# Attention with stick-breaking weights: the softplus of key blocks 2 and 3 is summed on VectorE, and one product serves both

## The reference, cut to what matters

```
neg_log_keep = jnp.where(mask, jax.nn.softplus(z), 0.0)
rcs = lax.cumsum(neg_log_keep, axis=3, reverse=True)
suffix = jnp.concatenate([rcs[..., 1:], jnp.zeros_like(rcs[..., :1])], axis=-1)
a = jnp.where(mask, jnp.exp(jax.nn.log_sigmoid(z) - suffix), 0.0)
return jnp.einsum('bhqk,bhkd->bhqd', a, vf)
```

## Time and profile before

| | us |
|---|---|
| median of 3 runs | 1982.65 (1981.83 to 1983.25) |
| the profiled execution | 1983.95 |
| its span | 1982.2 |
| TensorE busy | 1948.1 (98%) |
| VectorE busy | 1106.1 (56%) |
| ScalarE busy | 661.3 (33%) |
| GpSimd busy | 149.5 (8%) |
| mean granted TensorE clock | 0.993 |

### The profile page before, as it was taken

The page is one execution under the profiler, slowest core; times in us unless marked ns, Lnnn a source line. Parts: engine busy times, 40 slices in busy tenths (PEclk is TensorE's granted clock), DMA queues, the critical chain, the costliest instruction groups (busy, mean ns, idle before and its releaser), DMA issues.

```text
span 1982.2 us, 24091 instructions
## 1 busy us (share of the span) xinstructions
PE 1948.1 (98%) x9454; PEld 1568.1 (79%) x9454; DVE 1106.1 (56%) x1344; ACT 661.3 (33%) x742; POOL 149.5 (8%) x101
## 2 busy tenths in 40 slices
PE   6999999999999999999999999999999999999999
PEld 4888888876578888888888888888778788888887
DVE  3866564589887565633665533345569774333222
ACT  3422322242254323232432322223248743322211
POOL 0100000121411000001100000111012020000000
PEclk8999999999989999999999999999999999999999
DMA  9454544436413545433254422233235323222222
GB/s 394 163 211 171 206 167 162 161 103 183 125 59 133 212 170 201 167 123 101 107 212 172 188 99 76 99 119 114 85 93 137 112 85 106 85 106 85 88 97 91
DMA packets 50777, 275.88 MB, mean 139 GB/s; under 512 B 7456, under 2 KB 8096, under 8 KB 25760
## 3 DMA queue, kind: packets, MB, share of 16 engines
q1 hardware_dynamic: 47648, 270.87, 38.7%
q10 hardware_dynamic: 3072, 4.23, 0.9%
HBM read 251.94 MB, written 2.10 MB: 128 GB/s over the span
## 4 chain that ended last, share of the span: by engine, by line
PE 90%; DVE 4%; ACT 2%; DMA 2%; issue 1%; SPq 0%; ACTq 0%; DVEq 0%
PE ps L1420 27%; PE ps L1421 26%; PE ps L1422 26%; PE ps L1662 2%; PE ps L1441 2%; DMA stage<-ada_d 1%; PE ps L1796 1%; PE ps L1810 1%; PE ps L1782 1%; PE ps L1448 1%; DVE w L864 1%; PE ps L1549 1%; PE ps L1461 1%; PE ps L1460 1%; PE ps L1466 1%
## 5 line engine op out<-in xcount | busy, mean ns | idle before, releaser
L1420 PE MATMUL ps<-h_hi,w 128*128 128x512 f32 x1552 | 609.6, 393 | 0.1
L1422 PE MATMUL ps<-h_hi,w 128*128 128x512 f32 x1552 | 604.2, 389 | 0.0
L1421 PE MATMUL ps<-h_lo,w 128*128 128x512 f32 x1552 | 604.1, 389 | 0.0
L1420 PEld LDWEIGHTS ps<-h_hi,w 128*128 128x128 f32 x1552 | 291.3, 188 | 72.1 <-issue 11.4
L1422 PEld LDWEIGHTS ps<-h_hi,w 128*128 128x128 f32 x1552 | 291.3, 188 | 61.5
L1421 PEld LDWEIGHTS ps<-h_lo,w 128*128 128x128 f32 x1552 | 291.4, 188 | 58.8
L864 DVE TENSOR_TENSOR w<-raw,w 128x1408 fp32r<-128x1408 f32 (+1 forms) x104 | 198.8, 1911 | 208.8 <-ACT w L609 208.8
L609 ACT ACTIVATE w<-raw 128x1408 fp32r<-128x1408 f32 (+1 forms) x104 | 164.6, 1583 | 417.4 <-PE ps L1422 405.7
L1420 PE MATMUL ps<-g_hi,w 128*128 128x512 f32 x704 | 274.2, 390 | 0.0
L1422 PE MATMUL ps<-g_hi,w 128*128 128x512 f32 x704 | 273.9, 389 | 0.0
L1421 PE MATMUL ps<-g_lo,w 128*128 128x512 f32 x704 | 273.9, 389 | 0.0
(11 more groups left out here) (215 smaller groups left out, 1719.4 us busy)
## 6 DMA issues: line engine op xcount, KB each, us to landing
raw<-up_d SPq DMA_DIRECT2D x88, 1024.0 KB, 6.3
ada_raw<-ada_d SPq DMA_DIRECT2D x64, 1024.0 KB, 4.8
raw<-down_d SPq DMA_DIRECT2D x64, 704.0 KB, 4.1
raw<-mix_d SPq DMA_DIRECT2D x28, 1024.0 KB, 4.8
stage<-ada_d SPq DMA_DIRECT2D x12, 1024.0 KB, 21.1
stk<-parted SPq DMA_DIRECT2D x32, 256.0 KB, 4.4
stk<-parted SPq DMA_DIRECT2D x32, 128.0 KB, 2.3
u_blk<-u SPq DMA_DIRECT2D x48, 64.5 KB, 2.0
```

What stands on the lines that cost most here:

```text
L1420: pe.matmul(dst, a_hi_, b_hi_, start=start, stop=False, skip_group_check=True)
L1421: pe.matmul(dst, a_hi_, b_lo_, start=False, stop=False, skip_group_check=True)
L1422: return pe.matmul(dst, a_lo_, b_hi_, start=False, stop=stop, skip_group_check=True)
```

## The change

Three things are changed in the attention. The buffers of softplus become 128 columns wider (`QX` = 1408). In part 0 VectorE adds block 3 and the last 128 columns of block 2 into the new columns, after the softplus and before the cast; cast and low part then take 896 columns instead of 768. And in `suffix` the contributions of blocks 2 and 3 to block 1, and to block 0, come from one product of 256 columns per part, which reads the first 128 columns of block 2 and the 128 new columns (two runs of 128 with a gap between them), where there was one of 256 and one of 128. So part 0 has four products and part 1 three, each done for `sp_hi` and for `sp_lo`.

```diff
+QX = QL + P
+SPLIT = [slice(512, QX), slice(0, 512)]
...
-            sp_hi = ov("sp_hi", [P, QL], F32R)
-            ov("pad_c", [P, 3 * SLAB - 6 * S - QL])
-            sp_abs = ov("sp_abs", [P, 2, QL])
-            sp_lo = ov("sp_lo", [P, QL], F32R)
+            sp_hi = ov("sp_hi", [P, QX], F32R)
+            ov("pad_c", [P, 3 * SLAB - 6 * S - QX])
+            sp_abs = ov("sp_abs", [P, 2, QX])
+            sp_lo = ov("sp_lo", [P, QX], F32R)
...
                 dve.wait_ge(sp_done, 2 * t + p + 1)
+                if p == 0:
+                    f = sp_abs[:, t % 2, :]
+                    dve.tensor_tensor(f[:, QL:QX], f[:, QL - P:QL], f[:, 2 * S - P:2 * S], ALU.add).then_inc(both_done, 1)
+                    dve.wait_ge(both_done, t + 1)
                 if t >= 1:
                     dve.wait_ge(cum_done, 2 * t)
-                dve.tensor_copy(sp_hi[:, PIECE[p]], w).then_inc(sphi_done, 1)
+                w = sp_abs[:, t % 2, SPLIT[p]]
+                dve.tensor_copy(sp_hi[:, SPLIT[p]], w).then_inc(sphi_done, 1)
                 dve.wait_ge(sphi_done, 2 * t + p + 1)
-                dve.tensor_tensor(sp_lo[:, PIECE[p]], w, f32(sp_hi[:, PIECE[p]]), ALU.subtract).then_inc(splo_done, 1)
+                dve.tensor_tensor(sp_lo[:, SPLIT[p]], w, f32(sp_hi[:, SPLIT[p]]), ALU.subtract).then_inc(splo_done, 1)
...
-                    for c, later in (((1, 2), (1, 3), (2, 2), (2, 3)), ((0, 0), (0, 1), (0, 2), (0, 3)))[p]:
-                        last = pe.matmul(zps[:, span(base, c, P * later)],
-                                         con[:, 2 if later == c else 3, :],
-                                         part[:, span(0, later, P * later)],
-                                         start=False, stop=(part is sp_lo), skip_group_check=True)
+                    for c, later in (((2, 2), (2, 3)), ((0, 0), (0, 1)))[p]:
+                        pe.matmul(zps[:, span(base, c, P * later)], con[:, 2 if later == c else 3, :],
+                                  part[:, span(0, later, P * later)], start=False, stop=(part is sp_lo),
+                                  skip_group_check=True)
+                    behind = part[:, 2 * S:QX].rearrange("p (n q) -> p n q", n=3)[:, 0:3:2, :]
+                    last = pe.matmul(zps[:, span(base, 1 - p, 2 * P)], con[:, 3, :], behind, start=False,
+                                     stop=(part is sp_lo), skip_group_check=True)
```

More of the change, by code:

```diff
@@ L305, in trunk @@
         splo_done = sem("splo_done")
+        both_done = sem("both_done")
         cum_done = sem("cum_done")
```

## The result

The changed kernel takes 1989.6 us (median of 8, 1988.58 to 1990.08) against 1982.61 before (median of 8, 1981.83 to 1983.39): a ratio of 1.0032, 95% interval 1.0023 to 1.0040. It is slower, as forecast (1988.5). The profiled execution takes 1988.82 us, its span is 1987.0.

The account below looks back on a forecast made before the run. VectorE's queue was taken as the bound: 0.57 us late by head 2, plus 5.3 over ten heads, gives 5.87, and 5.8 after the last heads. 1982.65+5.8 = 1988.5 us, range 1985.4 to 1991.0.

Parts of the forecast that it names:

- VectorE is a second, full loop: Heads 2 to 13: VectorE has no idle time; two heads take 11.70 us before, 12.76 with the change.
- The price per head: VectorE, part 0: addition and its step 0.33 us, wider cast 0.066, wider subtraction 0.133; sum 0.53 us a head.
- GpSimd: Odd heads up to 11: the addition waits for GpSimd's subtractions as the cast did, so the whole added work still counts.
- rival (a): Heads 3, 5, 7, 9, 11: addition runs through or hides in GpSimd's work; +4.15 us, 1986.8 us; chance 0.12.
- Start: Heads 0 to 2: casts after head 0 stay, held by a transfer; low parts 0.53, 0.53 and 0.57 us late.
- Heads 3 to 12: VectorE has no slack, so ten heads at 0.53 us add 5.3; head 12's low part is 5.87 late.
- End: Heads 12 to 15: lateness 5.69 us after head 12, 6.04 after head 14; head 15 saves 0.24, leaving 5.8.
- TensorE's saving: Four fewer product steps of 0.06 us a head, 3.8 us over 16 heads; only the last 0.8 shows.
- (c): VectorE's new idle time on TensorE lowers its clock in two or three more stretches: about 2.5 us, 1991.0 us; chance 0.08.
- (b): TensorE is the bound and VectorE only follows, so the saving counts: -3.8 us, 1978.8 us; chance 0.05.
- (d): The addition on VectorE costs 0.10 to 0.15 us a head more: 12 heads, +1.5, 1990.0 us; chance 0.13.
- (e): TensorE's product with the gap costs 0.06 us more: +0.4 us in the last heads; no chance of its own.

Follow-up runs that it names:

- group 2: Two kernels with the new products, against before (stage 97.58 us): addition without wider cast and low part, stage 101.15 us; wider operations without addition, 99.47 us.
- after_again: The changed kernel as it is, run once more: stage 103.58 us, median 1989.18 us, ratio to before 1.0031.
- vector_only: Changed kernel with TensorE's old nine products given back, VectorE's new work kept: stage 104.07 us, median 1990.42 us, ratio to before 1.0036.
- products_only: Kernel before with the seven new products, block 3's share in blocks 0 and 1 left out, nothing new on VectorE: stage 96.78 us, median 1982.10 us.
- group 1: Each engine's side alone, against before: vector_only with VectorE's new work, +6.49 us in the stage; products_only with TensorE's seven products, -0.80 us.

## Why the prediction was right, point by point

- **VectorE is a second, full loop** that neither the busy shares nor the chain of before names. Right: two heads take 12.73 us (12.76 forecast), and the chain after is VectorE alone.
- **The price per head.** Addition 0.294 us (0.296), cast 0.627-0.560 = 0.067 (0.066), low part 1.092-0.958 = 0.134 (0.133), and a step of 0.034 (0.035). Right, and shown as terms in group 2.
- **GpSimd.** The addition took 1.02 to 1.03 us in the odd heads 1 to 11, and the cast after it was undisturbed (0.63): rival (a), +4.15 us, is out. The Trainium skill's rule ("SBUF — State Buffer", Who interferes with whom) that a VectorE instruction with two SBUF inputs contends with a GpSimd one that reads SBUF agrees with these rows (1.02 beside GpSimd, 0.29 without).
- **Start.** In head 0 the forecast put the casts at a fixed time, held by a transfer. In after, after_again and vector_only the transfer was no hold, and the casts came right after the low part, 0.36 us earlier in the stage than in before: head 1 was 0.16 late, not 0.53, and head 2 0.39 instead of 0.57. This term was too large by 0.2 to 0.4 us. Why the transfer held in before but not in these three is open.
- **Heads 3 to 12.** 5.58-0.39 = 5.19 us (5.3).
- **End.** The forecast let head 15 give 0.24 us back, since it "waits for nothing new". But VectorE's second low part of head 15 was 6.29 late like the first, and TensorE had to wait for it (it ends at 1575.88, the product that reads it starts at 1575.94): from the products with the values after head 14 (5.73 late) to the end the lateness grew by 0.27. This is the step that failed; it was 0.5 us too small. That the total is so near (6.00 against 5.8) is in part luck: an error of 0.3 at the start and in heads 3 to 12 and one of 0.5 at the end nearly cancel.
- **TensorE's saving.** Forecast 0.8 us of 3.8 on the path; products_only gives 0.80, and in the changed kernel it is 0.49 (vector_only).
- **TensorE's idle time** was to rise by 9.6 us; its waits rose by only 6.0 (5.0 to 11.0). The last section says where the rest is.
- **The clock.** The stretch of 3.4 us at the lower level (granted clock 0.50) that follows TensorE's wait in head 1 is there as in before; from 1489.8 to 1577 us the clock is 1.00, so there is no second one.
- **The rivals.** (a) and (c) are out by the above, (b) by products_only and vector_only, (d) by the 0.294, and (e) by the equal steps with and without the gap (group 1).
- **The time.** 1988.5 forecast, 1989.6 measured. The first comparison has 6.99 us between the medians, the second 5.80; the stage says 6.00, and this is the number that bears on the forecast's 5.8. What sets the stage's start in an execution is open.

## What to carry to other kernels

When three engines run in step, ask of each the time of one round of its own queue; an engine without a pause is a bound even where the chain of waits and the busy shares of the whole kernel do not name it. Work moved from TensorE to such an engine costs its full length in nearly every round (6.80 us here, 12.8 of 16 heads at 0.53), and what TensorE is relieved of becomes waiting (0.80 of 3.8 us came back). The same queue is where to look for gains: moving two casts so that GpSimd's work falls beside operations it does not block was worth 2.49 us in the changed kernel.

## What the runs showed that I had not expected

After a wait, the second product starts later behind the first than it does in a run. In the kernel after, TensorE's timeline has the same pair of products twice, first without and then after a wait:

```profile
1524.56 0.39 PE L1801 MATMUL ps<-sp_hi,con 128*128 128x512 f32 x1
1524.80 0.34 PE L1804 MATMUL ps<-sp_hi,con 128*128 128x256 f32 x2
...
1530.21 0.50 PE L1801 MATMUL ps<-sp_hi,con 128*128 128x512 f32 x1 [0.67 <-DVE sp_hi L1381]
1530.55 0.34 PE L1804 MATMUL ps<-sp_hi,con 128*128 128x256 f32 x2
```

The step is 0.24 us without and 0.34 with the wait, and the profile counts the 0.10 as busy. The groups of the stage's first product of part 0, high and low, before and then after (busy us, mean ns, idle before), show how often:

```profile
L1793 PE MATMUL ps<-sp_lo,con 128*128 128x512 f32 x16 | 7.6, 476 | 0.1
...
L1793 PE MATMUL ps<-sp_hi,con 128*128 128x512 f32 x16 | 6.5, 407 | 2.3 <-DVE sp_hi L1373 2.3
```

```profile
L1801 PE MATMUL ps<-sp_lo,con 128*128 128x512 f32 x16 | 8.1, 504 | 2.7 <-DVE sp_lo L1383 2.2
...
L1801 PE MATMUL ps<-sp_hi,con 128*128 128x512 f32 x16 | 7.4, 460 | 5.8 <-DVE sp_hi L1381 5.7
```

The means rise by 28 and 53 ns, which over 16 heads is 1.3 us of the 3.8 that appear neither as idle time nor as speed (the stage less TensorE's waits is 92.6 us in both kernels).

The rest lies on the other side of a wait. The last products ahead of one are counted to their own end, while in a run the next product starts before that. Six products of logits and the product after them in the kernel after, for two heads, with and without a wait between:

```profile
1553.98 1.02 PE L1790 MATMUL ps<-stk 128*128 128x384 f32 x6
1555.68 0.50 PE L1801 MATMUL ps<-sp_hi,con 128*128 128x512 f32 x1 [0.68 <-DVE sp_hi L1381]
...
1561.91 1.02 PE L1790 MATMUL ps<-stk 128*128 128x384 f32 x6
1562.77 0.39 PE L1801 MATMUL ps<-sp_hi,con 128*128 128x512 f32 x1
```

Without the wait the six take 1562.77-1561.91 = 0.86 us from start to start, with it 1.02 are counted as busy: 0.16 more. The waits number 8 in before and 23 in after. As an estimate from these rows, 15 x 0.16 = 2.4 us, and with the 1.3 that is 3.7 of the 3.8.
